# Projection weights visited back and forth, and the next input tile loaded later in the queue

## The reference, cut to what matters

```python
proj = rmsnorm(xf, norm_mix_g) @ w_in            # 1024 -> 2208 columns
p_mla, p_rw = proj[..., :MLA_COLS], proj[..., MLA_COLS:]
# rwkv_inputs: the token shift
shifted = jnp.concatenate([prev[:, None, :], p_rw[:, :-1]], axis=1)
xm = p_rw + (shifted - p_rw) * mu_shift
r, k, v = xm[..., :o], xm[..., o:2 * o], xm[..., 2 * o:3 * o]
wl, al, gl = ...                                  # low-rank inputs for decay, a, gate
# mla_kv_rows
c = rmsnorm(p_mla[..., Q_LORA:Q_LORA + KV_LORA], kv_norm_g)
kr = rope(rmsnorm(p_mla[..., Q_LORA + KV_LORA:MLA_COLS], kn_rope_g), pos)
```

## Time and profile before

| what | value |
|---|---|
| median of 3 runs | 1986.47 us |
| profiled execution, its own time | 1982.82 us |
| its span | 1981.0 us |
| PE busy | 1841.3 us (93%) |
| DVE, POOL, ACT busy | 1000.0, 688.0, 361.7 us |
| PE busy in slices 1 to 16 of 40 | 6 to 9 tenths |
| weight loads on q10 | 7344 packets, 76.88 MB, 11.2% of the DMA engines' span |
| `wsl<-in_w_in`, issue to landing, median | 7.9 us |
| `xt<-in_x_tiles`, issue to landing, median | 12.0 us |

### The profile page before, as it was taken

One profiled execution on the slowest core, in us unless ns is written; L12 is line 12 of the kernel. 1 busy time (PEld: TensorE's weight loads), 2 busy tenths in 40 slices (PEclk: granted clock), 3 DMA queues, 4 the chain that ended last, 5 costly groups with the idle time before them and its releaser, 6 DMA issues. The chain is left out here.

```text
span 1981.0 us, 33700 instructions
## 1 busy us (share of the span) xinstructions
PE 1841.3 (93%) x14303; PEld 1362.0 (69%) x14303; DVE 1000.0 (50%) x1742; ACT 361.7 (18%) x898; POOL 688.0 (35%) x495
## 2 busy tenths in 40 slices
PE   6799899999999796999989799999999999899998
PEld 3456566556566664555556488888888888688887
DVE  0657677677676785555533434343443443423522
ACT  1322332332323332333300100000000000000000
POOL 2543544544543453644500212222222221352622
PEclk9999999999999798999989899999999999899999
DMA  9545455554542101610031201111111111233331
GB/s 387 170 154 181 144 160 160 166 160 148 177 150 76 52 8 32 163 43 11 1 151 43 88 22 43 43 43 43 43 43 43 43 43 51 91 125 110 125 102 63
DMA packets 74071, 193.26 MB, mean 98 GB/s; under 512 B 19641, under 2 KB 48137, under 8 KB 66882
## 3 DMA queue, kind: packets, MB, share of 16 engines
q1 hardware_dynamic: 66578, 114.23, 18.2%
q10 hardware_dynamic: 7344, 76.88, 11.2%
HBM read 162.97 MB, written 20.44 MB: 93 GB/s over the span
## 5 line engine op out<-in xcount | busy, mean ns | idle before, releaser
L2241 PE MATMUL psum<-mixT,wA 128*128 128x264 f32 x1408 | 337.9, 388 | 6.3 <-DVE mixT L2431 4.8
L393 PE MATMUL psum<-wsl,xt 128*128 128x368 f32 x868 | 308.3, 496 | 5.2 <-ACT proj L869 4.1
L2241 PE MATMUL psum<-u_sum,wA 128*128 128x264 f32 x1232 | 299.0, 388 | 9.6 <-POOL wA L2381 9.6
L2241 PEld LDWEIGHTS psum<-mixT,wA 128*128 128x128 f32 x1408 | 269.2, 191 | 53.4 <-issue 5.3
L2241 PEld LDWEIGHTS psum<-u_sum,wA 128*128 128x128 f32 x1232 | 235.1, 191 | 50.1 <-POOL wA L2381 9.7
L393 PEld LDWEIGHTS psum<-wsl,xt 128*128 128x128 f32 x868 | 159.7, 196 | 105.9 <-issue 23.9
L2379 POOL TENSOR_TENSOR wA<-wA 128x512 f32<-128x512 f32 x22 | 27.9, 1267 | 401.1 <-DMA wA<-in_w_gate 203.3
L2241 PE MATMUL psum<-hid,wA 128*128 128x264 f32 x528 | 121.5, 386 | 2.1 <-DVE hid L2499 1.5
L2241 PEld LDWEIGHTS psum<-hid,wA 128*128 128x128 f32 x528 | 100.2, 190 | 19.9 <-issue 2.8
L2224 PE MATMUL psum<-mixT,wo 128*128 128x352 f32 x336 | 104.2, 474 | 7.0 <-PEq L2562 4.6
L2224 PEld LDWEIGHTS psum<-mixT,wo 128*128 128x128 f32 x336 | 66.0, 197 | 44.9 <-issue 8.3
(11 more groups left out here) (360 smaller groups left out, 2854.6 us busy)
## 6 DMA issues: line engine op xcount, KB each, us to landing
wsl<-in_w_in ACTq DMA_DIRECT2D x51, 1472.0 KB, 7.9
wA<-in_w_down SPq DMA_DIRECT2D x32, 704.0 KB, 4.1
wA<-in_w_gate SPq DMA_DIRECT2D x22, 512.0 KB, 4.3
wA<-in_w_up SPq DMA_DIRECT2D x22, 512.0 KB, 4.4
mixed<-proj SPq DMA_DIRECT2D x8, 784.0 KB
xt<-in_x_tiles SPq DMA_DIRECT2D x9, 512.0 KB, 12.0
wsl<-in_w_in SPq DMA_DIRECT2D x3, 1472.0 KB, 11.4
out_y<-hid SPq DMA_DIRECT2D x1, 4224.0 KB, 12.0
```

Of the source, the lines that this page charges most:

```text
L393: return pe.matmul(out, lhsT, rhs, start=start, stop=stop)
L2241: ins = pe.matmul(pb[bank][:, 0:NW], left(k), right(k), start=first and k == 0, stop=k == depth - 1, skip_group_check=not first)
```

## The change

The six pieces are visited in an order that alternates: an even tile computes columns 0, 1, 2, 3, 4, 5 and an odd tile 3, 4, 5, 0, 1, 2 (`columns`). After its first three pieces a tile loads the other three into the slots; the last three pieces load nothing, since what they leave in the slots is what the next tile begins with. Instead of 54 loads there are 3 + 27. PE's wait count for a slot follows (`slot_loads`). On SP, the load of the input tile f + 2 moves behind the store of tile t - 1 and the stores of the latents and key of tile f.

```diff
+    def columns(p, n):
+        return (n + IPC // 2 * (p % 2)) % IPC
+    def slot_loads(p, n):
+        return p + 1 + n // SLOTS
...
                 shift(f)
                 if f == LAST:
                     sample_loads()
-                if f + 2 < TILES:
-                    sp.wait_ge(s["ip_ps"], f * IPC + IPC)
-                    sp.dma_start(xt[f % 2][:, :, :], io.x_tiles[f + 2]).then_inc(s[f"x_in{f % 2}"], 16)
             if t >= 1:
                 store_rw(t - 1)
...
                     sp.dma_start(io.kr_p[a:a + P, :], kr[:, :]).then_inc(s["st_lat"], 16)
+                if f + 2 < TILES:
+                    sp.wait_ge(s["ip_ps"], f * IPC + IPC)
+                    sp.dma_start(xt[f % 2][:, :, :], io.x_tiles[f + 2]).then_inc(s[f"x_in{f % 2}"], 16)
                 sp.wait_ge(s["v_ok"], f + 1)
...
-                        pe.wait_ge(s[f"w_sl{at % SLOTS}"], 16 * (at // SLOTS) + 16)
+                        pe.wait_ge(s[f"w_sl{piece % SLOTS}"], 16 * slot_loads(p, piece))
-                        last = mm(pb[0][:, 0:IPW], xt[b][:, k, :], wsl[at % SLOTS][:, k, :], k == 0, k == KD - 1)
+                        last = mm(pb[0][:, 0:IPW], xt[b][:, k, :], wsl[piece % SLOTS][:, k, :], k == 0, k == KD - 1)
...
-            copy(proj[p % 2][:, n * IPW:(n + 1) * IPW], pb[0][:, 0:IPW], scale=rstd[p % 2][:, 0:1]).then_inc(s["p_ok"], 1)
-            if at + SLOTS < TILES * IPC:
-                act.dma_start(wsl[at % SLOTS][:, :, :], io.w_in[(at + SLOTS) % IPC]).then_inc(s[f"w_sl{at % SLOTS}"], 16)
+            w = columns(p, n) * IPW
+            copy(proj[p % 2][:, w:w + IPW], pb[0][:, 0:IPW], scale=rstd[p % 2][:, 0:1]).then_inc(s["p_ok"], 1)
+            if n < SLOTS:
+                act.dma_start(wsl[n][:, :, :], io.w_in[columns(p, n + SLOTS)]).then_inc(s[f"w_sl{n}"], 16)
```

## The result

| what | before | after |
|---|---|---|
| median, measured together (4 runs each) | 1985.31 us | 1956.03 us |
| span of the profiled execution | 1981.0 us | 1955.5 us |
| issue of tile 8's shift | 637.90 us | 606.12 us |
| from there to the end of the span | 1343.1 us | 1349.4 us |

The changed kernel is faster: 0.9857 times the old time, 95% interval 0.9837 to 0.9877, some 29 us of the median and 25.5 us of the two spans. The forecast was 1971.0 us with a range of 1960 to 1981. All times and ratios of this document are of fast runs; one run of the kernel before that took 10624.65 us, in the last group of the experiments, is left out.

What follows compares the result with a forecast made beforehand. PE, busy 93%, was taken to lose 24.9 us in transposes waiting for ACT behind a late shift. Gains of 9.4 (tiles 2 to 7), 4.0 (tile 1) and 2.1 (tile 0), 15.5 from 1986.5, gave 1971.0 us, range 1960 to 1981.

Steps and rivals of the forecast that it cites:

- Rival 1: The shift is slow by itself and lands no earlier; at most tile 0's gain, 1984 to 1986.5 us; chance 0.08.
- The landing: In tiles 1 to 7 the shift lands 7.30 us after its issue, as in tile 8, instead of about 12.
- The collision: POOL's mix stretches DVE's rotary key, so `T1h` starts 12.64 us after the shift's issue, as in tile 8.
- predicted wait of 2.4 us: New wait of PE for `T1h` in tiles 2 to 7, before the next matmuls; 1.15 of 3.52 us won.
- The clock: PE's clock falls in four of tiles 2 to 7, 1.27 us each; the six win 9.4 us (6.9 to 14.5).
- Tile 1: DVE's mix starts 2.72 us earlier and PE's clock has no reason to fall: 4.0 us won (1.15 to 4.8).
- Tile 0: Weight loads ahead of its shift go; PE comes to the transposes 2.08 us earlier: 2.1 us won (0 to 4.1).
- The input load: On SP, issued 13 to 14 us after the shift, with nobody waiting for it: worth nothing.
- Tile 8 and all behind keep their length: Tile 8 and all behind `layer_inputs` take as long as before the change.
- Rival 3: PE's clock never falls in tiles 2 to 7: 20.6 us won, 1965.9 us; inside the forecast's range, chance 0.66.
- Rival 4: POOL's mix misses the rotary key, no collision: 35.9 us won, 1950.6 us; chance 0.09, including anything between it and the forecast.
- Rival 2: The new wait costs PE's clock for long in tiles 2 to 7: 6.4 us slower, 1992.9 us; chance 0.05.

Runs made afterwards that it cites:

- kernel 1: The changed kernel with the input load put back on SP right behind the shift, so the alternating weights alone: 1953.7 us, ratio 0.9826 to the kernel before.
- kernel 2: The kernel before with only the input load moved, behind the stores of latents and key: 1985.65 us, ratio 0.9997.
- kernel 3: The changed kernel with one extra weight load per tile but the last, behind piece 5, just ahead of the shift: 1979.95 us, ratio 0.9979.
- kernel 4: The changed kernel with the same 8 extra weight loads issued behind piece 3, some 20 us ahead of the shift: 1956.4 us, ratio 0.9838.
- kernel 7: The changed kernel with the write of `T1h` done two more times in the steps of tiles 2 to 7: 1969.15 us, ratio 0.9909.
- kernel 8: The changed kernel with the write of `T1h` done three more times in the steps of tiles 2 to 7: 1972.3 us, ratio 0.9929.
- kernel 9: The changed kernel with three more writes of `T1h` in the step of tile 7 alone: 1955.9 us, ratio 0.9845.
- kernel 5: The changed kernel with DVE's rotary key moved behind the additions `sig` and `av`: 1948.0 us, ratio 0.9806 to the kernel before.
- kernel 6: The changed kernel with the sample rows' cache loads moved behind the stores of tile 8's latents and key: 1956.4 us, ratio 0.9845.

## Why the prediction was wrong in size

**The cause of the late shift: right.** The weight load ahead of it was the cause and the input load innocent (kernels 1 to 4). Rival 1, a shift that is slow by itself, fell.

**The landing: the step that failed.** I took tile 8's 7.30 us for tiles 1 to 7; they have 5.85 to 5.97. I had called tile 8 "a picture" of the others, one tile with its own surroundings. Everything after it was carried over from the same tile, and shifted with it. As an estimate, put 5.85 for 7.30 into the prediction's own working: `T1h` starts 12.64 - 7.30 = 5.34 us behind the landing and is ready at 5.85 + 5.34 + 0.69 = 11.9 us, PE waits 0.9, the transposes start at about 15.0, and a tile wins, without a fall, 2.5 + 1.27 = 3.8 us; 3.74 were measured in tile 3. Two more errors cancel in this: the transposes really started 0.45 later, and a piece of 0.42 is missing (below). Step by step:
- *The collision* is real, but what I carried over was its distance from the issue, 12.64 us to `T1h`. It belongs to the landing: POOL's four operations last 5.24 us (255.96 to 261.20), and DVE is held up until they are through. With 0.73 us for the last three operations of the key, 5.85 + 5.24 + 0.73 = 11.82 us to `T1h`, as the trace has it.
- *PE came later.* With the collision this early it also hit L1367, on which PE's transposes L456 wait. PE stood at the matmuls for `T1h` 11.78 us behind the issue, not 10.95; 0.55 of these 0.83 us are the wait for L1367. Both together turned the predicted wait of 2.4 us into 0.78. The matmuls began at 12.56 instead of the 13.33 of the forecast.
- *The clock* did not fall in any of tiles 2 to 7. By kernels 7 and 8 the estimate for the clock is possible for a wait of 2.4 us; its input was wrong.

Tile 3's 3.74 us then come out in three pieces, each measured from the issue: the transposes started at 15.45 us instead of 17.51 (2.06 won, 1.15 forecast), 0.42 on the way from there to the four matmuls (2.41 us before, 1.99 after; the prediction put this at nothing), and 1.27 in these, at full clock. Six tiles at that are 22.5 us; the forecast had 9.4 and an upper bound of 14.5. Tile 2 had a double fall before and won 5.25. The bound was no bound, because it went by one start of `T1h` alone.

**A reading under the clock: wrong.** I called the forecast wait longer than both rows of the clock. PE's stop at 1024 us, before the change, lasted 2.41 us, as long as the wait that I forecast, and the clock fell behind it:

```profile
1026.37 3.85 PE L2224 MATMUL psum<-mixT,wo 128*128 128x352 f32 x7 [2.41 <-DMA wo<-in_w_out]
```

**Why the key is stretched: shown, but not by the rows I named.** I took L1521's 0.69 us in both tiles as support: one input in PSUM, not stretched. In neither did it run beside a POOL operation (in tile 8 POOL ended at 650.27, L1521 began at 650.54), so these two rows don't test it. L1535 at 257.64 above does: it has its input in PSUM, ran beside L1182 and kept 0.69.

**Tile 1: 4.0 forecast, 5.1 measured,** above its bound of 4.8. **Tile 0: 2.1 forecast, 2.4 measured,** but this can't be told from chance: up to tile 1's issue the same program took 106.8 us in kernel 7 and 109.8 in kernel 9, and kernel 3, with the load ahead of the shift again, 109.2. That DVE's wait of the earlier trace rows for the shift is gone, is shown: its mix there has no wait before it.

**The input load: right.** Issued 13.2 us behind the shift, landed 4.1 us later, and nobody waits for it.

**"Tile 8 and all behind keep their length": 6.3 us longer in the profiled execution; the cause is open.** The work and the shift's landing there are the same as before (7.41 and 7.30 us). In another stretch of it PE ran at half clock, and in a chain of small dependent matmuls. Six kernels with the same program from tile 8 on (the changed one, 1, 4, 7, 8 and 9) took 1343.3 to 1349.4 us for it, each in one execution. That is what the clock makes of one program; that the change made it longer isn't shown. The medians don't show it either: they differ by 29.3 us, and the tiles 1 to 7 alone won 29.4.

**The rivals.** Rival 3, a clock that never falls, was right on the clock, but its 1965.9 us had the late `T1h` in it. Rival 4 came nearer than the forecast (1950.6 against 1971.0, measured 1956.0), and its reason was wrong: the collision is there, and kernel 5, which takes the key out of it, is 8 us faster still by the medians, with 2.2 us won in the tiles 1 to 7 of its profile. That it came near is luck. Rival 2 did not come. In the profiled executions the sum before tile 8 (31.8 us against 15.5) was wrong by more than the 25.5 us between the spans show.

## What to carry to other kernels

Where one place of the old trace is to stand for the new state of others, ask what it has of its own, and anchor each later offset to the event that causes it (the landing), not to the start of the row. A DMA that something waits for should not be issued behind a large load of another queue; look at what was issued in the last microseconds before it. Where whole executions of one kernel differ by 9 us, don't read a difference of 5 or 6 us in one profiled execution as an effect of an edit; put it into the range, and profile more than one.

## What the runs showed of the hardware

- The load of 1472 KB on ACT's queue held up a transfer that was issued 0.6 us later on SP's almost wholly: 0.7% of the DMA engines for the shift against 98.6% for the weights over 5 us in kernel 3, so 12 us to landing instead of 5.9. The same load issued behind piece 3 did nothing to it (5.79 to 6.01 us).
- Most DVE operations of 128x16 to 128x256 with their inputs in SBUF that ran beside POOL's mixes or level mask ended when one of POOL's operations did: 0.17 to 0.48 us became 1.0 to 1.6. Size mattered little. One that started before POOL's operation, or with it, could keep its time (L1366 at 255.85: 0.49 us). The Trainium skill says in "SBUF — State Buffer", under "Who interferes with whom", that a VectorE instruction with two SBUF inputs contends with a GpSimd instruction that reads SBUF. The trace agrees: L1531, with one input in PSUM, took 0.69 us in every case, also in the 16 up to 700 us that ran beside a POOL operation.
- PE's clock after a wait of the tiles 2 to 7: no fall in 21 tiles with a wait of 0.8 us for `T1h` (the changed kernel, 4, 6 and 9); two in four after a wait of 1.6 us for the latents (4, 5, 6 and 7); two in five after 2.2 us (7); five in six after 3.0 (8); six in six after the old waits of 3.4 to 3.8. Two waits of equal length (2.95 and 2.97 us) had different outcomes, so the length of the wait alone doesn't decide. The same program from tile 8 on took 1343.3 to 1349.4 us, in six kernels with one execution each, with the clock low in other stretches.
